# Attention of a fused block: scaling moved to GpSimd, values in plain fp32 on alternating halves of the array

## The reference

```python
def attend(blk):
    qn, qr = blk
    s = (jnp.einsum('bqhd,bkhd->bhqk', qn, k_nope)
         + jnp.einsum('bqhd,bkd->bhqk', qr, k_rope))
    pr = jax.nn.softmax(s.astype(jnp.float32) * scale, axis=-1).astype(v.dtype)
    return jnp.einsum('bhqk,bkhd->bqhd', pr, v)
```

## Time and profile before

| | |
|---|---|
| Time, median of 3 runs | 3148.76 us (3148.34 to 3150.01) |
| The profiled execution | 3148.84 us, of which the span is 3147.0 |
| TensorE, matmuls | busy 3099.2 us, 98% of the span, 14840 instructions |
| TensorE, weight loads | 2531.3 us, 80% |
| VectorE | 2360.8 us, 75% |
| ScalarE | 1254.2 us, 40% |
| GpSimd | 90.2 us, 3% |
| Granted TensorE clock | 0.998 of full speed |

### The profile page before, as it was taken

One profiled execution on the slowest core, in us unless ns is written; L12 is line 12 of the kernel. 1 busy time (PEld: TensorE's weight loads), 2 busy tenths in 40 slices (PEclk: granted clock), 3 DMA queues, 4 the chain that ended last, 5 costly groups with the idle time before them and its releaser, 6 DMA issues.

```text
span 3147.0 us, 38018 instructions
## 1 busy us (share of the span) xinstructions
PE 3099.2 (98%) x14840; PEld 2531.3 (80%) x14840; DVE 2360.8 (75%) x4053; ACT 1254.2 (40%) x1952; POOL 90.2 (3%) x113
## 2 busy tenths in 40 slices
PE   8999999999999999999999999999999999999998
PEld 6887888877988888888878888888777688788887
DVE  6777767778859678778598767667798689789736
ACT  4233323335242456656243223223365534534414
POOL 0000000000000002332000000000000000000000
PEclk9999999999999999999999999999999999999999
DMA  3222212213333450003211111111111311122242
GB/s 131 74 74 76 78 61 67 68 67 128 104 95 134 142 192 26 14 21 137 99 54 55 53 54 53 54 47 54 67 54 52 114 70 70 41 76 101 80 167 74
DMA packets 89249, 250.15 MB, mean 79 GB/s; under 512 B 8560, under 2 KB 24816, under 8 KB 87536
## 3 DMA queue, kind: packets, MB, share of 16 engines
q1 hardware_dynamic: 89072, 247.73, 22.8%
HBM read 203.65 MB, written 44.04 MB: 79 GB/s over the span
## 4 chain that ended last, share of the span: by engine, by line
PE 90%; DVE 6%; ACT 3%; issue 1%; DMA 0%; POOL 0%; DVEq 0%; SPq 0%; POOLq 0%; ACTq 0%
PE PS L570 88%; PE PS L575 2%; DVE X L2245 1%; DVE WS L2237 1%; DVE XS L2245 1%; DVE HELD L2299 1%; DVE X L2237 1%; ACT XS L1352 0%; DVE XSf L2237 0%; ACT XSf L1352 0%; DMA RAW<-in_W 0%; ACT WS L1352 0%; ACT TMP L1352 0%; DVE TMP L2237 0%; DVE HELD L2237 0%
## 5 line engine op out<-in xcount | busy, mean ns | idle before, releaser
L570 PE MATMUL PS<-XS,WS 128*128 128x512 f32 (+1 forms) x6480 | 1512.2, 390 | 20.6 <-DVE XS L2237 9.4
L570 PEld LDWEIGHTS PS<-XS,WS 128*128 128x128 f32 x6480 | 1207.5, 188 | 297.8 <-issue 26.9
L570 PE MATMUL PS<-HS,WS 128*128 128x512 f32 x2208 | 512.6, 391 | 3.1 <-DVE TMP L2237 2.7
L570 PEld LDWEIGHTS PS<-HS,WS 128*128 128x128 f32 x2208 | 415.2, 188 | 93.6 <-DVE TMP L2237 3.5
L2237 DVE TENSOR_TENSOR WS<-RAW,WS 128x512 fp32r<-128x512 f32 (+1 forms) x398 | 347.2, 881 | 173.1 <-ACT WS L1352 172.5
L1352 ACT ACTIVATE WS<-RAW 128x512 fp32r<-128x512 f32 (+1 forms) x398 | 307.7, 779 | 401.2 <-PE PS L570 350.1
L2237 DVE TENSOR_TENSOR X<-PS,X 128x512 f32<-128x512 f32 x272 | 184.3, 689 | 101.7 <-PE PS L570 101.7
L2237 DVE TENSOR_TENSOR TMP<-TMP,PS 128x512 f32<-128x512 f32 x304 | 203.7, 683 | 61.2 <-PE PS L570 58.4
L570 PE MATMUL PS<-T,WS 128*128 128x512 f32 x960 | 230.6, 389 | 0.0
L570 PEld LDWEIGHTS PS<-T,WS 128*128 128x128 f32 x960 | 180.2, 188 | 37.4
L1352 ACT ACTIVATE TMP<-PS 128x512 f32<-128x512 f32 x144 | 85.0, 596 | 290.5 <-PE PS L570 273.8
(11 more groups left out here) (337 smaller groups left out, 3663.6 us busy)
## 6 DMA issues: line engine op xcount, KB each, us to landing
RAW<-in_W SPq DMA_DIRECT2D x263, 512.0 KB, 3.3
RAWX<-in_W SPq DMA_DIRECT2D x30, 512.0 KB, 3.2
DC<-TMP SPq DMA_DIRECT2D x32, 256.0 KB, 2.1
X<-in_xT SPq DMA_DIRECT2D x8, 512.0 KB, 8.7
DX<-X SPq DMA_DIRECT2D x2, 2048.0 KB, 9.1
DCZ<-CA SPq DMA_DIRECT2D x8, 512.0 KB, 4.3
DGA<-TMP SPq DMA_DIRECT2D x16, 256.0 KB, 2.1
DGB<-TMP SPq DMA_DIRECT2D x16, 256.0 KB, 2.8
```

Of the source, the lines that this page charges most:

```text
L570: done = d.matmul(out, l, r, start=first, stop=last)
```

## The change

GpSimd no longer scales the identity. It multiplies the tile's weights themselves (PROB, 128 x 1024, in place) by the reciprocals (`scale_rows`), and the turn waits for this, one iteration later than before; what follows the turn moves by an iteration too. The spread of the reciprocals (`row_sums`) and the multiplication by it in `o_out` go. The turned weights PT and the values VH are stored in plain fp32 without a low part: ScalarE copies the first half of a turned tile, VectorE the second, and likewise for the values. The product with the values is eight plain fp32 matmuls of 64 weight columns, even ones into rows 0 to 63 and odd ones into rows 64 to 127 of the bank; the addition of both in `o_out` stays. VH now holds all eight heads, so the values of heads 4 to 7 are made in iterations 29 to 32, one block each, and no longer wait for val 15.

```diff
-    VH = at("VH", 128, [128, 8, 4, 2, 64], F32R)
+    VH = at("VH", 128, [128, 8, 8, 64], F32)
-    PT = at("PT", 160, [128, 2, 2, 8, 256], F32R)
+    PT = at("PT", 160, [128, 2, 8, 256], F32)
...
             def turn(n):
                 for g in range(2):
-                    e.wait_ge(ac("ex", n), dma("const")("cols"))
-                    e.wait_ge(ve("pt", n - 1, g) if n else ve("vh", 0, 2 + g))
+                    e.wait_ge(po("pn", n), dma("const")("cols"))
+                    e.wait_ge(turned_out(n - 1, g) if n else values_out(0, 2 + g))
...
-            def row_sums(j):
-                use = ("val", j)
-                m = misc.take(use, (ve, "ot", j))
-                sums = PS[0:64, m, 256:512]
-                e.wait_ge(po("wt", 2 * j + 1), *misc.free(use))
-                mms([(sums[:, 128 * q:128 * q + 128], ones[:, 0:64], weight(2 * j + q), True, True) for q in range(2)])
...
             def values(j):
                 hd, p, use = j // 4, j % 2, ("val", j)
-                out, items = PS[:, misc.slot.get(use, 0), 0:256], []
-                for n in range(8):
-                    v = VH[:, n, hd % 4]
-                    both = (out, v.rearrange("p a d -> p (a d)"), PT[:, p, 0, n, :], n == 0, n == 7)
-                    rest = (out[0:64], v[:, 0], PT[:, p, 1, n, :], False, False)
-                    items += [rest, both] if n == 7 else [both, rest]
-                e.wait_ge(ac("pt", 2 * j + 1, 1), ve("pt", 2 * j + 1, 1), ve("vh", hd // 4, 3))
-                mms(items).then_inc(*mm.inc(*use))
+                out = PS[:, misc.take(use, (ve, "ot", j)), 0:256]
+                e.wait_ge(turned_out(2 * j + 1, 0), turned_out(2 * j + 1, 1), values_out(hd // 4, 2), values_out(hd // 4, 3),
+                          *misc.free(use))
+                mms([(out[64 * (n % 2):64 * (n % 2) + 64], VH[:, n, hd, :], PT[:, p, n, :], n < 2, n > 5)
+                     for n in range(8)]).then_inc(*mm.inc(*use))
...
-            for n in range(67):
+            for n in range(68):
                 hd, i = n // 8, n % 8
-                if 2 <= n < 66:
-                    turn(n - 2)
+                if 3 <= n < 67:
+                    turn(n - 3)
                 if n < 64:
                     scores(n)
-                if n == 36:
-                    row_sums(16)
-                if n >= 4 and n % 2 == 0:
-                    values((n - 4) // 2)
+                if n >= 5 and n % 2:
+                    values((n - 5) // 2)
...
-                if n in (34, 35):
-                    for q in ((0,), (1, 2, 3))[n - 34]:
-                        heads_v(1, q)
-                if n >= 3 and n % 2 == 1 and n < 66 and n != 35:
-                    row_sums((n - 3) // 2)
+                if 29 <= n < 33:
+                    heads_v(1, n - 29)
...
-        def scale_ident(n):
-            e.wait_ge(ve("ri", n), dma("const")("cols"), *([mm("val", n // 2 - 2)] if n > 3 else []))
-            d.tensor_scalar(weight(n), ident[:], stat(n)[3], None, op0=ALU.mult).then_inc(*po.inc("wt", n))
+        def scale_rows(n):
+            e.wait_ge(ve("ri", n), ac("ex", n))
+            d.tensor_scalar(PROB[n % 3], PROB[n % 3], stat(n)[3], None, op0=ALU.mult).then_inc(*po.inc("pn", n))
```

More of the change, by code:

```diff
@@ L494, in z_part @@
         return Z[:, g8].rearrange("p s (g c) -> p g s c", c=16)[:, par:par + 7:2]
-    def weight(n):
-        return TMP[:, 4, 128 * (n % 4):128 * (n % 4) + 128]
     def k_high(hd, h):
@@ L517, in values_bank, with values_rows, values_out, turned_out @@
         return PS[:, misc.slot.get(("hv", b, i), 0) if b else 4 + i, :]
+    def values_rows(b, i):
+        return VH[:, 2 * i:2 * i + 2, 4 * b:4 * b + 4, :], values_bank(b, i).rearrange("p (n h d) -> p n h d", n=2, h=4)
+    def values_out(b, i):
+        return ve("vh", b, i) if i % 2 else ac("vh", b, i)
+    def turned_out(n, g):
+        return ve("pt", n, 1) if g else ac("pt", n, 0)
     def hs_free(name, f):
@@ L1010, in heads_v @@
                 if b:
-                    misc.take(use, (ve, "vh", b, i))
+                    misc.take(use, (ve if i % 2 else ac, "vh", b, i))
                     e.wait_ge(*misc.free(use))
@@ L1026, in scores @@
                 if n < 2:
-                    e.wait_ge(ve("yb", 7, 1), ve("vh", 0, n))
+                    e.wait_ge(ve("yb", 7, 1), values_out(0, 0), values_out(0, 1))
                 else:
@@ L1093, in attention @@
                     banks.ends[2 + 2 * (n % 2) + g] = ((ac, "ex", n),)
-                banks.ends[6 + g] = ((ac, "pt", 63, g), (ve, "pt", 63, g))
+                banks.ends[6 + g] = ((ve if g else ac, "pt", 63, g),)
             banks.at += (2 - banks.at) % 8
@@ L1794, in v_out @@
             def v_out(b, i):
-                e.wait_ge(mm("hv", b, i), mm("val", 15) if b else mm("yb", 7, 1))
-                act(VH[:, 2 * i:2 * i + 2, :, 0, :], values_bank(b, i).rearrange(
-                    "p (n h d) -> p n h d", n=2, h=4), ACT.Copy).then_inc(*ac.inc("vh", b, i))
+                if i % 2 == 0:
+                    e.wait_ge(mm("hv", b, i), mm("yb", 7, 1))
+                    act(*values_rows(b, i), ACT.Copy).then_inc(*ac.inc("vh", b, i))
                 if b and i == 3:
@@ L1819, in turn_out @@
                 p, j, o = (n // 2) % 2, n // 2, 128 * (n % 2)
[L1820 to L1827, removed]
+                e.wait_ge(mm("tr", n, 0))
+                if j > 1:
+                    e.wait_ge(mm("val", j - 2))
+                else:
+                    e.wait_ge(ac("cq", 2), ve("cq", 2), ve("kr", 1, 1))
+                act(PT[:, p, 0:4, o:o + 128], PS[:, 6, :].rearrange("p (k q) -> p k q", q=128), ACT.Copy).then_inc(
+                    *ac.inc("pt", n, 0))
             def exps(n):
@@ L1856, in attention @@
                 v_out(0, i)
[L1857 to L1861, removed]
+            for n in range(68):
+                if n >= 6 and n % 2 == 0:
+                    o_out((n - 6) // 2)
+                if 3 <= n < 67:
+                    turn_out(n - 3)
                 if 1 <= n < 65:
@@ L1864, in attention @@
                 hd, i = (n - 1) // 8, (n - 1) % 8
-                if n in (58, 60, 62):
-                    o_split((n - 58) // 2)
+                if n in (59, 61, 63):
+                    o_split((n - 59) // 2)
                 if n and hd < 7:
@@ L1871, in attention @@
                         k_out(hd + 1, i - 3)
[L1872 to L1875, removed]
+                if 30 <= n < 34:
+                    v_out(1, n - 30)
+                if n == 66:
                     o_split(3, (0,))
@@ L3031, in v_out @@
             def v_out(b, i):
-                e.wait_ge(ac("vh", b, i))
-                low(VH[:, 2 * i:2 * i + 2, :, 1, :], values_bank(b, i).rearrange(
-                    "p (n h d) -> p n h d", n=2, h=4), VH[:, 2 * i:2 * i + 2, :, 0, :]).then_inc(*ve.inc("vh", b, i))
+                if i % 2:
+                    e.wait_ge(mm("hv", b, i), mm("yb", 7, 1))
+                    d.tensor_copy(*values_rows(b, i)).then_inc(*ve.inc("vh", b, i))
                 if b and i == 3:
@@ L3059, in turn_out @@
             def turn_out(n):
[L3060 to L3064, removed]
+                p, j, o = (n // 2) % 2, n // 2, 128 * (n % 2)
+                e.wait_ge(mm("tr", n, 1))
+                if j > 1:
+                    e.wait_ge(mm("val", j - 2))
+                else:
+                    e.wait_ge(ac("cq", 2), ve("cq", 2), ve("kr", 1, 1))
+                d.tensor_copy(PT[:, p, 4:8, o:o + 128], PS[:, 7, :].rearrange("p (k q) -> p k q", q=128)).then_inc(
+                    *ve.inc("pt", n, 1))
             def o_split(m, hs=(0, 1)):
@@ L3086, in attention @@
                 v_out(0, i)
-            for n in range(67):
+            for n in range(68):
                 if 1 <= n < 65:
                     row_max(n - 1)
-                if n >= 5 and n % 2 == 1:
-                    o_out((n - 5) // 2)
                 if 2 <= n < 66:
                     normal(n - 2)
-                    turn_out(n - 2)
-                if n in (59, 61, 63):
-                    o_split((n - 59) // 2)
+                if n >= 6 and n % 2 == 0:
+                    o_out((n - 6) // 2)
+                if 3 <= n < 67:
+                    turn_out(n - 3)
+                if n in (60, 62, 64):
+                    o_split((n - 60) // 2)
                 hd, i = (n - 1) // 8, (n - 1) % 8
@@ L3102, in attention @@
                         k_out(hd + 1, i - 3)
[L3103 to L3106, removed]
+                if 30 <= n < 34:
+                    v_out(1, n - 30)
+                if n == 67:
                     o_split(3, (0,))
@@ L3632, in gpsimd @@
             hd, i = n // 8 + 1, n % 8
-            scale_ident(n)
+            scale_rows(n)
             if hd < 8 and i < 2:
```

5 lines of the change are left out of this document (1 added, 4 removed).

## The result

The changed kernel takes 3157.28 us (median of 8 runs, 3155.91 to 3158.81) against 3148.56 in the same session: 1.0027 times the time before, interval 1.0017 to 1.0037. It is slower by 9 us, clear of noise. The forecast was 3129. The profiled execution took 3158.81 us, the profiled one before 3148.84.

The account below looks back on a forecast made before the run. TensorE was taken to bound the kernel, a pair falling from 7.13 to 6.50 us. From 3148.84 us: -20.2 (pairs), -3.0 (waits), +2 (GpSimd delays), +1 (start), +0.5 (end) = -19.7, so 3129; range 3116 to 3156.

Parts of the forecast that it names:

- the price of the scaling: GpSimd's scaling of one 128x1024 tile: 1.37 us from the cast's slope and a fixed part of 0.50.
- rival 1: GpSimd's scaling sets the pace and turns wait for it: 3170 us at 3.65 us a scaling, 3247 at 4.84; chance 0.11.
- The second estimate: GpSimd's scaling by the skill page: 1.03 cycles an element at 1.2 GHz, also giving 1.37 us.
- Row sums: On TensorE, the row sums and their effect on neighbouring groups go: 0.73 us a pair, 23.4 us over 32.
- Values: TensorE's product with the values, eight fp32 products on alternating halves: 1.98 us a pair, 0.10 dearer than before.
- the two prices for the switch: Entering and leaving a values group on TensorE's array halves: 0.14 or 0.29 us, with 0.23 taken between them.
- The waits around the values of heads 4 to 7: In the head that makes these values, 3.0 us of waiting was expected to go.
- The loop: From scores through GpSimd's scaling and turn to later scores, over two tiles: 4.18 us plus the scaling's duration.
- rival 2: GpSimd's scaling takes 2.54 us, by the subtractions' slope: loop 4 us, other GpSimd operations about 22, kernel 3153; chance 0.07.
- Rival 3: The array halves do not overlap when accumulating: values 3.73 us, pair 8.25, kernel 3182; chance 0.05.
- rival 4: TensorE pays nothing for the switch and GpSimd never delays it: pair 6.27 us, kernel 3119; chance 0.09.
- rival 5: GpSimd and VectorE hinder each other at SBUF: 7 us, kernel 3136; chance 0.13 together with other small delays.

Follow-up runs that it names:

- e1: The changed kernel, but GpSimd scales only the first 512 of a tile's 1024 weight columns, the rest left unscaled; 3129.42 us.
- e2: The changed kernel, but GpSimd scales only the first 128 of a tile's 1024 weight columns, the rest left unscaled; 3125.85 us.
- e8: The changed kernel with full scaling, but GpSimd's q and k parts of heads 2 to 7 and its weight splits cut to 64 columns; 3146.18 us.
- e3: The changed kernel with the whole scaling moved from GpSimd to VectorE, nothing left out; 3131.59 us.
- e7: The changed kernel with the scaling divided, VectorE taking the first 512 columns of a tile and GpSimd the other 512; 3131.97 us.
- e4: The changed kernel with a fourth buffer for the weights and the turn four tiles behind the scores instead of three; 3140.69 us.

## Why the prediction was wrong

**The step that failed** is the price of the scaling: "The operation reads one tensor, as the cast does, so the cast's slope is the nearest row: I take 1.37". It is 2.85 us, over the 2.3 that the loop could hide, and the turns wait for it: the first of the stated signs of being wrong came true. The second, a wait before most turns, did not quite: 29 of 64 wait. The per-element price is 2.50 ns, near the two-input subtraction's 2.16 and not the cast's 0.85, and the fixed part 0.28, near the casts' 0.17 and not 0.50. So the operation costs like one that computes, though it reads one tensor; why, no run here shows. I also had to give the operation a fixed part three times that of every other GpSimd operation, and named this in rival 1 as evidence without letting it weigh.

**The second estimate.** The one by "GPSIMD Engine Reference", section 3.1, of the Trainium skill gave 1.37 as well; measured are 2.50 ns an element, at the page's 1.2 GHz three cycles and not 1.03. For this operation the measurement decides. Page and cast agreed, and I took this for two pieces of evidence; neither had the operation in it. With the Trainium skill's rule in "TensorEngine Tiling (Array Packing)", Key Properties, that a change of the tiling mode drains the engine, the trace agrees in kind: 0.09 us ahead of a values group and 0.06 behind it in e1.

**What held.** Row sums: 0.73 us a pair gone. Values: 2.03 for 1.98; the upper of the two prices for the switch, 0.29, would have met it. The pair 6.56 for 6.50. The waits around the values of heads 4 to 7: before, their head took 9.3 us more than a plain one (41.9 and 32.6). Now they are made in head 3, which has k products too; in e2 it takes 39.0 against 33.2 for the other heads with k, 5.8 more. That is 3.5 us less, for the 3.0 forecast. The loop: 6.99 for 7.03. The sum with a hidden scaling: 3129.4 in e1 for 3129 (between e2 and e1, at D = 1.37, a straight line gives an estimate of 3128.7).

**The rivals.** The outcome lies between rival 2 (D = 2.54, 3153) and rival 1 (3.65, 3170): the line between them gives 3158 at 2.85, and 3157.3 was measured. That it fits to 1 us is luck in part: rival 2 put 4 us on the loop and 22 on the other GpSimd operations, while e8 shows that of the 31.4 us only 11.1 go when those are cut. Rival 1's mechanism is what happened: GpSimd's scaling sets the pace. The bounds were right, the chances were not, 0.18 for the two together, and the range ended at 3156. Rival 3 is refuted by 1.88 us a group, rival 4 by the switch that costs 0.28 us (2.03 less 1.75), and rival 5 holds only where VectorE itself scales.

**Not foreseen** was the clock. Rival 1 counted gaps at their length; two of the five longest also lost 3.4 us at the lower level behind them.

## What to carry to other kernels

Before a work step moves to another engine, its price there must come from a row of the same operation in two sizes; between neighbours of another kind take the dear one when the step sits in a loop. Here the time was flat as long as the loop had slack (0.96 us more of D cost 3.6 us) and steep once it had none (0.64 us more cost 17). Compare the new step with the slack of the loop it closes, then add what else the queue holds between two of them. A wait that leaves TensorE idle for two microseconds can cost again behind it, at the lower clock; the windows of the profile show whether it did.

## What the runs showed of the hardware

- GpSimd's fp32 tensor_scalar with one scalar per partition: 0.28 us and 2.50 ns an element, over 128 to 1024 columns; the same on VectorE 0.75 us for 1024 with no GpSimd operation beside it (42 times in e3).
- VectorE's fp32 scaling and GpSimd's operations lengthen each other: in e3 a cast of 1.04 us becomes 1.31 on average and VectorE's scaling of 0.75 up to 1.89; in e7 a half scaling of 1.56 becomes 1.80.
- Plain fp32 products on the two column halves overlap fully when they alternate (16 records of 256 columns in 1.88 us) and for about a third of the time when four products follow four (2.79).
- The granted clock fell to 0.50 for some 4 us behind two gaps of TensorE of 2.26 and 2.27 us in the changed kernel and stayed at 1.00 behind three of 2.22 to 2.27. In e8 it fell behind gaps of 1.96 and 1.73 us (at 1213 and 1466), while a gap of 1.75 in the stage before, and one of 2.26 in e4, left it at 1.00.
